# A feed-forward's gate and up projections as Strassen's 2x2 blocks, with the down pass moved behind them

## The reference

```python
D_FF = -(-8 * D_MODEL // (3 * 256)) * 256      # 2816
h2 = ada_norm(x, norm2_g[l], sh2, sc2)
gt, up = jnp.split(h2 @ w_gu[l], 2, axis=-1)
x = x + g2 * ((jax.nn.silu(gt) * up) @ w_down[l])
```

## Time and profile before

| | |
|---|---|
| median of 3 runs | 2940.02 us |
| the profiled execution | 2940.54 us, its span 2938.8 us |
| TensorE busy, share of the span | 2866.2 us, 98% |
| VectorE busy | 1748.4 us, 59% |
| ScalarE busy | 1034.6 us, 35% |
| GpSimd busy | 446.1 us, 15% |
| mean granted TensorE clock | 0.992 |

### The profile page before, as it was taken

The page is one execution under the profiler, slowest core; times in us unless marked ns, Lnnn a source line. Parts: engine busy times, 40 slices in busy tenths (PEclk is TensorE's granted clock), DMA queues, the critical chain, the costliest instruction groups (busy, mean ns, idle before and its releaser), DMA issues.

```text
span 2938.8 us, 40297 instructions
## 1 busy us (share of the span) xinstructions
PE 2866.2 (98%) x16452; PEld 2270.6 (77%) x16452; DVE 1748.4 (59%) x1932; ACT 1034.6 (35%) x1343; POOL 446.1 (15%) x508
## 2 busy tenths in 40 slices
PE   6998999999999999999999999999999999999999
PEld 4886667778888888888877888888888887777777
DVE  6557638763755555543467848668768345455463
ACT  4124445652411111111235424334434114444462
POOL 3012010001211111110101103021212002223240
PEclk8999999999999999999999999999999999999999
DMA  7454011101333333321115233243531322212121
GB/s 244 144 167 108 6 30 31 30 23 43 103 119 107 102 107 108 113 93 50 43 45 151 74 89 113 79 125 103 182 114 51 108 86 65 72 37 70 39 87 58
DMA packets 248122, 258.66 MB, mean 88 GB/s; under 512 B 14431, under 2 KB 208656, under 8 KB 247968
## 3 DMA queue, kind: packets, MB, share of 16 engines
q1 hardware_dynamic: 223280, 179.70, 20.0%
q0 software_dynamic: 19008, 59.19, 6.8%
q10 hardware_dynamic: 5680, 17.58, 1.5%
HBM read 223.41 MB, written 30.65 MB: 86 GB/s over the span
## 4 chain that ended last, share of the span: by engine, by line
PE 90%; DVE 4%; ACT 3%; issue 2%; DMA 1%; SPq 1%; POOL 0%; ACTq 0%; DVEq 0%; POOLq 0%
PE PU L1080 18%; PE PU L1082 17%; PE PU L1081 17%; PE PM L1870 3%; PE PM L1882 2%; PE PU L1858 2%; PE PU L1096 2%; PE PU L1097 2%; PE PU L1098 2%; PE PM L1902 2%; PE PU L1469 2%; PE PM L1904 2%; PE PM L1903 2%; PE PU L1391 2%; PE PM L1483 1%
## 5 line engine op out<-in xcount | busy, mean ns | idle before, releaser
L1080 PE MATMUL PU<-hH,w_hi_t 128*128 128x512 f32 x1792 | 706.1, 394 | 0.9 <-DVE w_lo_t L2727 0.6
L1082 PE MATMUL PU<-hH,w_lo_t 128*128 128x512 f32 x1792 | 698.3, 390 | 0.0
L1081 PE MATMUL PU<-hL,w_hi_t 128*128 128x512 f32 x1792 | 697.7, 389 | 0.0
L1082 PEld LDWEIGHTS PU<-hH,w_lo_t 128*128 128x128 f32 x1792 | 335.1, 187 | 72.4
L1080 PEld LDWEIGHTS PU<-hH,w_hi_t 128*128 128x128 f32 x1792 | 335.3, 187 | 72.0 <-issue 1.7
L1081 PEld LDWEIGHTS PU<-hL,w_hi_t 128*128 128x128 f32 x1792 | 335.5, 187 | 68.6
L2727 DVE TENSOR_TENSOR w_lo_t<-w_raw,w_hi_t 128x1024 fp32r<-128x1024 f32 x180 | 235.6, 1309 | 215.9 <-ACT w_hi_t L2016 208.0
L2016 ACT ACTIVATE w_hi_t<-w_raw 128x1024 fp32r<-128x1024 f32 x166 | 174.2, 1049 | 411.5 <-PE PU L1082 327.8
L3283 DVE SCALAR_TENSOR_TENSOR xT<-PU,mod,xT 128x1024 f32<-128x1024 f32 x120 | 153.8, 1282 | 158.6 <-PE PU L1082 158.6
L3627 DVE TENSOR_TENSOR_SCAN s_keep<-s_keep,zero 128x128 f32<-128x128 f32 (+7 forms) x128 | 182.0, 1423 | 76.3 <-POOL s_keep L1035 76.3
L1035 POOL TENSOR_SCALAR_AFFINE_SELECT s_keep<-s_keep 128x128 f32<-128x128 f32 x128 | 94.2, 743 | 464.6 <-ACT s_keep L2613 464.2
(11 more groups left out here) (518 smaller groups left out, 5072.9 us busy)
## 6 DMA issues: line engine op xcount, KB each, us to landing
ada_w<-in_ada_w_dram POOLq DMA_DIRECT2D x64, 384.0 KB, 4.0
w_raw<-in_w_gu_dram SPq DMA_DIRECT2D x44, 512.0 KB, 3.8
w_raw<-in_m_in_w_dram SPq DMA_DIRECT2D x40, 512.0 KB, 3.9
ada_w<-in_w_ada_dram POOLq DMA_DIRECT2D x32, 512.0 KB, 4.6
seg<-decay_sums SPq DMA_DIRECT2D x32, 512.0 KB, 4.3
w_raw<-in_w_down_dram SPq DMA_DIRECT2D x22, 512.0 KB, 3.3
w_raw<-in_w_in_dram SPq DMA_DIRECT2D x17, 512.0 KB, 3.9
ada_w<-in_w_ada_dram SPq DMA_DIRECT2D x16, 512.0 KB, 15.0
```

Of the source, the lines that this page charges most:

```text
L1080: mm(PU[0:width, up, half, :], whi, aH[:, k, cols], start=k == 0, stop=False)
L1081: mm(PU[0:width, up, half, :], whi, aL[:, k, cols], start=False, stop=False)
L1082: last = mm(PU[0:width, up, half, :], wlo, aH[:, k, cols], start=False, stop=k == kt - 1)
```

## The change

For the inner tiles 2 to 21, a pair of a gate tile and an up tile is computed as one 2x2 block product. The weights' blocks are even and odd feature tiles by gate and up; the activations' blocks are even and odd feature tiles by the first and second 512 tokens. Strassen's scheme, in Winograd's form, replaces 8 block products by 7 and needs sums of blocks on both sides and additions of the results. A product is called a phase: 4 feature tiles x 3 = 12 matmuls of 512 tokens into one bank of PSUM; phases 4, 5 and 6 add to a bank that still holds phase 0, 2 or 3.

- The sums of the activations (16 differences, from the raw `row_tiles`) are formed once, on VectorE, after the gating of tile 0, and split. The sums of the weights (4 per pair) are formed by VectorE in every pair; then each phase's weights are split (`phase_high` on ScalarE, `phase_low` on VectorE) into a ring of 4 slots. A high part may overwrite a slot once the phase of 4 places earlier is done.
- VectorE combines the phases' results in seven instructions of 512 columns; ScalarE moves the first gate half and applies silu to both halves.
- Finished tiles are stored to memory (`gated_tiles`), on ScalarE's DMA queue, which also issues the loads of the pair after next (two of 512 KB).
- The down pass comes behind all pairs, in five groups of four tiles and one of two; the tiles are loaded back and split again. The first group's tiles 0 and 1 are split inside the last pair, tiles 2 and 3 behind it.
- The modulation slabs are halved (512 columns), two jobs per four pairs, issued by SyncE; the last four jobs have full slabs, lie in the down pass and are issued by GpSimd.
- Tiles 0 and 1 keep their old units.

The diff, cut to its core:

```diff
+            def phase(i, r, q):                                    # TensorE
+                slot = phase_slot(7 * r + q)
+                pe.wait_ge(gu_low, GU_LOW + 28 * i + 7 * r + q + 1)
+                if q in (1, 2, 3):
+                    pe.wait_ge(t_ready, T_READY + (4, 8, 16)[q - 1])
+                if q in (0, 4):
+                    pe.wait_ge(gu_moved, GU_MOVED + 8 * i + 2 * r + q // 4)
+                elif q > 1:
+                    pe.wait_ge(gu_added, GU_ADDED + 20 * i + 5 * r + {2: -1, 3: 0, 5: 2, 6: 3}[q])
+                bank = PM[:, {0: 0, 1: 1, 2: 2, 3: 3, 4: 0, 5: 2, 6: 3}[q], :]
+                for k in range(4):
...
+                    mm(bank, gu_hi[slot][:, k, :], high, start=first, stop=False, skip_group_check=check)
+                    mm(bank, gu_hi[slot][:, k, :], low, start=False, stop=False, skip_group_check=check)
+                    last = mm(bank, gu_lo[slot][:, k, :], high, start=False, stop=k == 3, skip_group_check=check)
+                last.then_inc(gu_done, 1)
+            with counted(pe, 4, [(job, 2)]) as i:
+                phases_body(i, 1)
+            phases_body(4, 0)
+            for g in range(D_GROUPS):
+                _, high, low = down_rows(g)
+                tiles = min(4, FT - 4 * g)
+                pe.wait_ge(f_act, 4 * g + tiles)
...
+            sp.wait_ge(t_formed, T_FORMED + 12)                    # SyncE
+            gate_up_rows(0)
+            sp.wait_ge(raw_scaled, 4)
+            sp.dma_start(scr_f[0, :, :], f_first[:, 1, :]).then_inc(f_stored, 16)
+            sp.wait_ge(unit_free[1], D_UNIT0 // 2)
+            sp.dma_start(scr_f[1, :, :], f_second[:, :]).then_inc(f_stored, 16)
+            sp.wait_ge(f_stored, F_STORED + 32)
+            gate_up_rows(1)
...
+            def phase_high(i, r, q):                               # ScalarE
+                n = 7 * r + q
+                if q == 0:
+                    act.wait_ge(gu_landed[(r + 1) % 2], GU_LANDED + 32 * (2 * i + r // 2 + 1))
+                elif q in (1, 2, 6):
+                    act.wait_ge(gu_summed, GU_SUMMED + 16 * i + 4 * r + {1: 2, 2: 3, 6: 4}[q])
+                act.wait_ge(gu_done, GU_DONE + 28 * i + n - F_SLOTS + 1)
+                af(gu_hi[phase_slot(n)][:, :, :], phase_rows(r, q), ACT.Copy).then_inc(gu_high, 1)
...
+                    act.wait_ge(f_gated, F_GATED + 8 * i + 2 * r + 2)
+                    act.dma_start(scr_f[bass.ds(4 * i + r + 2, 1), :, :].rearrange("o p t -> (o p) t"), f_out[:, :]).then_inc(f_stored, 16)
...
+            for k in range(4):                                     # VectorE, at the entry
...
+                V.tensor_tensor(t1, even[:, b2_], even[:, b1], ALU.subtract).then_inc(t_formed, 1)
+                V.tensor_tensor(t3, odd[:, b2_], even[:, b2_], ALU.subtract).then_inc(t_formed, 1)
+                ve.wait_ge(t_formed, T_FORMED + 4 * k + 1)
+                V.tensor_tensor(t2, odd[:, b2_], t1, ALU.subtract).then_inc(t_formed, 1)
+                ve.wait_ge(t_formed, T_FORMED + 4 * k + 3)
+                V.tensor_tensor(t4, odd[:, b1], t2, ALU.subtract).then_inc(t_formed, 1)
...
+                    phase_low(i, r, 4)                             # VectorE, in a pair
+                    if not ending:
+                        weight_sum(i, r + 1, 1)
+                        weight_sum(i, r + 1, 2)
+                    half_slab(7 * r)
+                    ve.wait_ge(gu_done, done + 2)
+                    ve.wait_ge(gu_moved, GU_MOVED + 8 * i + 2 * r + 1)
+                    tt(mid, PM[:, 1, :], mid, ALU.add).then_inc(gu_added, 1)
+                    phase_low(i, r, 5)
...
```

More of the change, by code:

```diff
@@ L677, in _, with gate_up @@
             w_dn = a["w_down"].rearrange("o (k p) c -> p (o k) c", p=P)
[L679 to L684, removed]
+            def gate_up(t, up):
+                panel(w_gu[:, :, t * P + up * DFF:(t + 1) * P + up * DFF], KD, P)
             def token_rows(n):
@@ L2081, in _, with h_high @@
             ht = Tally()
-            def h_high(sh, tiles=range(KD), over=None):
+            def h_high(sh, tiles=range(KD), over=None, rows=None):
                 for k in tiles:
@@ L2353, in _ @@
             up0 = uc.at(1)
-            h_high(m("sh2", 0, 8), range(3), over=up0)
-            for n, dst in enumerate((f_silu, f_prod)):
+            h_high(m("sh2", 0, 8), range(3), over=up0, rows=row_tiles)
+            for n in range(2):
                 rp_, rn = uc.at()
@@ L2363, in _ @@
-            act.wait_ge(raw_scaled, 4)
-            af(f_hi[:, 0, :], f_prod[:, 0, :], ACT.Copy).then_inc(f_hi_s, 1)
-            up = Tally(1)
-            def gate(t, ahead=False):
-                if not ahead:
-                    split()
-                p = unit()
-                free(af(f_silu[:, t, :], unit_ps(p), ACT.Silu))
-            def high(t, upu):
-                act.wait_ge(unit_free[upu[0]], upu[1] + 1)
-                up.next()
-                af(f_hi[:, t, :], f_prod[:, t, :], ACT.Copy).then_inc(f_hi_s, 1)
+            af(f_first[:, 0, :], f_first[:, 0, :], ACT.Silu, bias=small[:, 44:45]).then_inc(raw_gate, 1)
@@ new lines, in _, with tiles_high @@
+            used.next(KD - 1)
+            unit()
+            skip()
+            phase_high(0, 0, 2)
+            for k in range(4):
+                token_sum_high(2, k)
+            phase_high(0, 0, 3)
+            def tiles_high(g, which=range(4)):
+                raw, high, _ = down_rows(g)
+                for k in which:
+                    if g:
+                        act.wait_ge(f_landed[g % 2], F_LANDED + 64 * (g // 2) + (64 if g in (1, 3) else 32))
+                    else:
+                        act.wait_ge(f_landed[0] if k < 2 else f_pair, F_LANDED + 32)
+                    af(high[:, k, :], raw[:, k, :], ACT.Copy).then_inc(f_hi_s, 1)
@@ L2379, in passed @@
+            with act.Fori(0, 4) as i:
+                highs_body(i)
+            highs_body(4, last=True)
+            tiles_high(0, range(2, 4))
             def passed(units):
@@ new lines, in _, with tiles_low @@
+            phase_low(0, 0, 2)
+            for k in range(4):
+                token_sum_low(3, k)
+            for k in range(4):
+                token_sum_low(2, k)
+            weight_sum(0, 0, 4)
+            phase_low(0, 0, 3)
+            fh = Tally()
+            def tiles_low(g, which=range(4)):
+                raw, high, low = down_rows(g)
+                for k in which:
+                    ve.wait_ge(f_hi_s, fh.next())
+                    V.tensor_tensor(low[:, k, :], raw[:, k, :], high[:, k, :].bitcast(F32), ALU.subtract).then_inc(f_act, 1)
```

565 lines of the change are left out of this document (369 added, 196 removed).

## The result

The changed kernel took 2913.51 us (median of 4 runs, 2912.8 to 2918.41) against 2939.62 us for the kernel before (4 runs); the ratio is 0.9912, its 95% interval 0.9895 to 0.9929. So it is about 0.9% faster, clear of the noise; the forecast was 2917. The profiled execution took 2912.8 us (span 2911.0), 27.7 less than that of before; the sum of the prediction was 23.0 less.

The account below looks back on a forecast made before the run. TensorE bounds the feed-forward: 128x512 matmuls times their pitch. Terms -54.4 + 1.6 + 1.0 + 18.8 + 10.0 = -23.0 us, from 2940.5 profiled to 2917.5; forecast median 2917, range 2904 to 2935.

Parts of the forecast that it names:

- column jobs: TensorE's column jobs in the feed-forward: 12 instead of 8, each 0.27 us plus some 0.15 in slower successors, +1.6 us.
- 140 phase starts: In the loop over the 20 pairs: starting 140 phases costs TensorE 1 us in all.
- entry: From the old units to the first pair's phases: VectorE's sums, row load and low clock delay TensorE, +18.8 us.
- joint to the down pass: Between last phase and first down matmul: wait of 7.0 us for tile splits, plus 3 for half clock, +10.0 us.
- What goes: In the 20 pairs: 84 matmuls each instead of 96, 240 fewer at 0.227 us, -54.4 us.
- VectorE in the loop: Per pair VectorE needs 14 to 16 us of TensorE's 19.0, so the loop is charged nothing for it.
- the walk through a pair: VectorE's order within one pair: hand-over margins 3.4 to 5.6 us; only the column job is narrow, reduction 18, wanted 19.0.
- cheap joints: Rival at the loop's two ends: rows land at once, no clock losses; entry 11, joint 6, total 2906 us; chance 0.12.
- phase starts that cost 0.25: Rival in the loop: each of 140 phase starts loses 0.25 us, 35 us in all, 2951 us; chance 0.05.
- Dearer pairs: Rival in the loop: each pair costs 0.8 us more, through column job and ScalarE's queue, 2933 us; chance 0.08.
- VectorE's pace: Rival in the loop: VectorE sets the pace, a pair takes 22.8 us, 76 us more, 2993 us; chance 0.05.
- The rule against the change: VectorE instructions never overlap: loop carries 16 us per pair, still hidden; entry some 2 us more, 2919 us.

Follow-up runs that it names:

- the two experiments on it: Each against the changed kernel: tiles 2 and 3 split sooner in the last pair, 2911.18 us; 28 unread matmuls filling TensorE's wait before the down pass, 2913.66 us.

## Why the prediction was right, step by step

| step | forecast | measured |
|---|---|---|
| 240 matmuls | -54.4 | -54.4 (0.2267 us of pitch in both) |
| column jobs | +1.6 | +1.6 (4 more at 0.40) |
| 140 phase starts | +1.0 | 0.0 |
| entry | +18.8 | +18.0 (28.9 to phase 4, less 4 x 2.72) |
| joint to the down pass | +10.0 | +9.4 (6.95 and 2.5 of clock) |
| small joints of the old stage | 0 | -1.4 |
| stage | -23.0 | -26.9 |
| before and behind it | 0 | -1.1 and +0.2 |

- **What goes** was exact: all 1680 matmuls of the phases are there, at the old pitch.
- **VectorE in the loop**: the estimate of 14 to 16 us per pair was good (264.39 us in 360 are 14.0 per 19.05), and the walk through a pair found the right narrow place, the column job. The margins of 3.4 to 5.6 us per hand-over can't be spent, though: four more instructions (2.4 us) in a pair already cost 7.4 us in all, most of it at the column jobs, whose margin is 1.2 us (forecast 1.0) and not 3.4. With seven, the loss also moved to the next pair when its first place was relieved, and a walk through one pair by itself can't show that.
- **The entry** was right in its chain and off by 0.8 us in its sum, with errors on both sides that partly cancel. The old units end 1.15 us sooner in this trace than in that of before, so times are counted from their end: rows issued at 2.3 us (forecast 2.3), usable 5.7 us later (6.0), phase 0 at 10.2 (10.5), phase 3 at 24.5 (25.0). The rows of the second pair cost nothing where 1.0 was counted. The clock behind the gap ahead of phase 3 cost 1.7 where 1 was. The fit in the Trainium skill, "DMA: Bandwidth & Descriptors", section "Anatomy of one DMA", gave the estimate of 4.4 us for the rows, and 5.7 were measured. The section gives its fit for DMAs that GpSimd issues, and SyncE issues these, so this says that the fit was used out of its place, not that it is wrong there.
- **The joint**: E+7.0 was forecast and 6.95 measured; the two experiments on it show both halves, queue and clock.
- **The term that was missed**: the stage of before spent 5.1 us on column jobs and small joints, and the prediction charged the new column jobs but did not credit the old joints, one of which stands in the earlier trace rows with 1.3 us (a wait for VectorE's addition to `xT`); behind the new down pass none is left. That, the phase starts, the joint and the entry are nearly all of the 3.9 us by which the stage came out shorter. The last 0.9 lie outside it and can't be told from chance, since these parts of a trace vary by more from run to run. The four terms all erred the same way, by 0.6 to 1.4 us each.
- **Rivals**: cheap joints (entry 11, joint 6) and phase starts that cost 0.25 are refuted by the trace. Dearer pairs and VectorE's pace did not happen, but the first sets in with four more instructions per pair, and the second with GpSimd at work. For that the prediction's 22.8 us per pair stands against 21.9 to 23.0 measured, half of two pairs, and its 1.03 us per instruction against a mean of 1.01.
- **The rule against the change** (no overlap of VectorE's instructions): starts 0.61 apart at a length of 0.69, as 792.54 and 793.15 above, so the trace goes on disagreeing with the rule as the prediction gives it. The Trainium skill, "VectorE: DVE Perf Modes", section "The DRAIN you can't avoid", has the exception too, which the prediction left out: an instruction that is not held starts earlier.

## What to carry to other kernels

A change that trades TensorE's matmuls for VectorE's instructions pays inside a loop where VectorE is busy three quarters of the time and no hand-over comes late; its price lies at the two ends, where the new chain isn't covered by matmuls, so sum up these chains instruction by instruction. Then split what an end waits for: loading sooner and starting on the tiles that are ready gave back 11.7 us of a price of 27.4. Spare time read as an average is not a margin; the narrowest hand-over is one. Work moved to GpSimd beside VectorE's two-input instructions is not free.

## What was not expected of the hardware

- A wait of 2.6 us on TensorE cost as much clock as one of 6.8 (first 24 matmuls 8.48 and 7.93 us, full pace 5.44), one of 0.43 cost 0.1 us (5.57), and behind waits of 3.0 us phase 3 took 4.3 to 4.45 us in most traces and 2.85 in one. Behind the same wait of 6.8 us, the 24 took 7.33 to 8.15 us in six traces.
- How much GpSimd slows VectorE depends on what it does: 0.69 became up to 1.2 us, and 1.01 in the mean, beside additions of 256 columns of 1.02 us each, and 1.7 to 1.8 beside subtractions of 512 columns of 1.99 us. VectorE's instructions that read PSUM stayed at 0.68.
